# Two transformer blocks on one core: the unit after next rounded between the token tiles, and up products with channels on partitions

## What is computed

```python
def rmsnorm(x, w):
    xf = x.astype(jnp.float32)
    y = xf * lax.rsqrt(jnp.mean(xf * xf, axis=-1, keepdims=True) + EPS)
    return (y * w.astype(jnp.float32)).astype(x.dtype)

def conv_ffn(h, w_up, conv_w, conv_b, w_down):
    u = causal_depthwise_conv(h @ w_up, conv_w, conv_b)
    g, val = jnp.split(u, 2, axis=-1)
    return (jax.nn.silu(g) * val) @ w_down

def swiglu(h, w_gu, w_down):
    gate, up = jnp.split(h @ w_gu, 2, axis=-1)
    return (jax.nn.silu(gate) * up) @ w_down
```

## Time and profile before

| | |
|---|---|
| median of 3 runs | 998.97 us (998.82 to 999.09) |
| the profiled execution | 998.76 us |
| its span, first to last instruction | 997.0 us |
| TensorE, weight loads, VectorE, ScalarE, GpSimd busy | 98%, 82%, 62%, 52%, 7% |
| mean granted clock of TensorE | 0.998 |

### The profile page before, as it was taken

How to read it: one execution, slowest core, us unless ns; L and a number is a source line. 1 busy time by engine, 2 the same in 40 slices (tenths; PEclk the granted TensorE clock), 3 DMA queues, 4 the chain that set the end, 5 groups by cost and what they waited for, 6 DMA issues and landing times.

```text
span 997.0 us, 13465 instructions
## 1 busy us (share of the span) xinstructions
PE 975.3 (98%) x5011; PEld 821.8 (82%) x5011; DVE 616.8 (62%) x770; ACT 518.3 (52%) x748; POOL 66.9 (7%) x98
## 2 busy tenths in 40 slices
PE   7999999999999999999999999999999999999996
PEld 6888888787878888888788789999899878888885
DVE  5645454765665454556678787675553766666766
ACT  6443444565563434455458286545442475555555
POOL 3300000000100000000001623000000000000000
PEclk9999999999999999999999999999999999999999
DMA  9855555532446555555444333234652526465541
GB/s 322 279 190 190 184 195 177 203 126 106 124 150 213 194 185 185 193 172 186 169 156 148 117 130 127 85 127 147 231 172 85 169 89 235 141 205 173 180 157 43
DMA packets 110113, 166.01 MB, mean 167 GB/s; under 512 B 5684, under 2 KB 83796, under 8 KB 109940
## 3 DMA queue, kind: packets, MB, share of 16 engines
q1 hardware_dynamic: 108040, 160.45, 48.1%
q0 software_dynamic: 1872, 4.93, 1.5%
q10 hardware_dynamic: 160, 0.07, 0.0%
HBM read 164.38 MB, written 1.05 MB: 166 GB/s over the span
## 4 chain that ended last, share of the span: by engine, by line
PE 88%; ACT 4%; DVE 4%; POOL 2%; issue 1%; DMA 0%; POOLq 0%; ACTq 0%; DVEq 0%
PE ps L1988 26%; PE ps L1990 25%; PE ps L1989 25%; ACT w_hi L610 1%; DVE w_lo L1291 1%; ACT xT_hi L668 1%; PE ps L2298 1%; PE ps L2197 1%; PE ps L2204 1%; DVE arena L1755 1%; PE ps L2272 1%; PE ps L2012 1%; PE ps L2536 1%; ACT xs L640 1%; PE ps L2694 1%
## 5 line engine op out<-in xcount | busy, mean ns | idle before, releaser
L1291 DVE TENSOR_TENSOR w_lo<-raw,w_hi 128x2048 fp32r<-128x2048 f32 (+1 forms) x141 | 322.4, 2296 | 151.7 <-ACT w_hi L610 151.6
L1988 PE MATMUL ps<-w_hi,xT_hi 128*128 128x512 f32 (+2 forms) x898 | 349.2, 389 | 6.4 <-DVE w_lo L1291 2.6
L1990 PE MATMUL ps<-w_hi,xT_lo 128*128 128x512 f32 (+2 forms) x898 | 339.9, 379 | 0.0
L1989 PE MATMUL ps<-w_lo,xT_hi 128*128 128x512 f32 (+2 forms) x898 | 339.5, 378 | 0.0
L610 ACT ACTIVATE w_hi<-raw 128x2048 fp32r<-128x2048 f32 (+1 forms) x141 | 265.7, 1897 | 66.1 <-PE ps L1990 56.8
L1988 PEld LDWEIGHTS ps<-w_hi,xT_hi 128*128 128x128 f32 x898 | 169.2, 188 | 39.9 <-issue 4.5
L1990 PEld LDWEIGHTS ps<-w_hi,xT_lo 128*128 128x128 f32 x898 | 168.9, 188 | 32.2
L1989 PEld LDWEIGHTS ps<-w_lo,xT_hi 128*128 128x128 f32 x898 | 169.3, 189 | 30.6 <-issue 1.4
L1988 PE MATMUL ps<-w_hi,hT_hi 128*128 128x512 f32 x224 | 87.8, 392 | 0.0
L1989 PE MATMUL ps<-w_lo,hT_hi 128*128 128x512 f32 x224 | 87.4, 390 | 0.0
L1990 PE MATMUL ps<-w_hi,hT_lo 128*128 128x512 f32 x224 | 87.4, 390 | 0.0
(11 more groups left out here) (303 smaller groups left out, 1051.2 us busy)
## 6 DMA issues: line engine op xcount, KB each, us to landing
raw<-in_ffn_w_gu SPq DMA_DIRECT2D x86, 512.0 KB, 4.7
raw<-in_ffn_w_down SPq DMA_DIRECT2D x44, 512.0 KB, 3.9
raw<-in_w_ffn_up SPq DMA_DIRECT2D x44, 512.0 KB, 5.2
raw<-in_w_in SPq DMA_DIRECT2D x38, 512.0 KB, 4.7
raw<-in_w_out SPq DMA_DIRECT2D x24, 512.0 KB, 3.9
raw<-in_w_ffn_down SPq DMA_DIRECT2D x22, 512.0 KB, 4.4
raw<-in_w_mem_k SPq DMA_DIRECT2D x8, 512.0 KB, 4.0
raw<-in_w_mem_v SPq DMA_DIRECT2D x8, 512.0 KB, 4.7
```

The source lines that it names most:

```text
L1291: TTn(w_lo[HOME[k]][:, 0:n], raw[k % RING][:, 0:n], w_hi[HOME[k]][:, 0:n].bitcast(F32), ALU.subtract).then_inc(resid, 1)
L1988: pe.matmul(out_, lh, rh, start=first, stop=False, **kw)
L1989: pe.matmul(out_, lh, rl, start=False, stop=False, **kw)
L1990: return pe.matmul(out_, ll, rh, start=False, stop=last, **kw)
```

## The change

**Seams.** At the four seams the split of unit k+2 is taken from behind the wait for `rstd`. ScalarE does it between the squares of tile 0 and the eviction of tile 1, VectorE behind its part of tile 1. f0, the very first layer, stays. A one-column Silu is put on ScalarE ahead of wout's end.

**Convolution layer.** Chunk 0 stays. From chunk 1 on `conv_up` computes the up products with a 128x128 block of weights stationary and the 256 tokens moving, so the result has channels on partitions (channel blocks 0 and 2 in bank 0, 1 and 3 in bank 1) and no transposes follow. The factor now varies along the free dimension, so it is needed as a row on every partition: VectorE writes the two diagonals of `rstd` and a matrix of ones, TensorE multiplies them behind chunk 0's transposes (`factor_row`), ScalarE copies the row (`r_row`). VectorE multiplies banks 0 and 1 by the row into `u_s` (two instructions of 128x512 each chunk), and the taps read `u_s`. `gu_ps` is raised when bank 0 is complete, in the middle of the second unit. ScalarE's write of `hT_hi` now waits for the down products of the chunk before.

```diff
+                    if t == 0:
+                        split(U0[name] + 2)
...
                 squares(after, (0,))
+                split(U0[after] + 2)
                 turned_tile(after, 1)
...
-                if f or peeled != 0:
+                if peeled != 0:
                     split(k + 2, j)
...
-                for t in range(TT):
+                for t in range(TT if not conv or peeled == 0 else 0):
...
+                if conv and peeled == 0:
+                    act.wait_ge(r_ps, 1)
+                    act.activation(r_row, ps[:, 6, 0:S], ACT.Copy).then_inc(r_ready, 1)
...
+                    if n:
+                        act.wait_ge(unit_used, 3 * j + (k + 3))
                     act.activation(hT_hi[:, :, :], act_s[:, :, :], ACT.Copy).then_inc(hT_hi_done, 1)
...
+            act.activation(rec1[:, 0:1], neg_half[:, 0:1], ACT.Silu)
             post_and_norm("wout", "f1")
...
+                if conv and peeled == 0:
+                    nc.vector.tensor_scalar(ones, ident, 0.0, 1.0, ALU.mult, ALU.add).then_inc(diag_ready, 1)
+                    for t in range(TT):
+                        scale_rows(diag[:, t, :], ident, rstd[:, t, 0:1]).then_inc(diag_ready, 1)
...
+                    for p in range(2 if peeled != 0 else 0):
+                        if p == 0:
+                            dve.wait_ge(gu_ps, j + (fc + 1))
+                        else:
+                            dve.wait_ge(unit_used, 3 * j + (k + 2))
+                        TTn(u_s[:, p::2, :], ps[:, p, :].rearrange("p (a b) -> p a b", a=2), bh(r_row, 2),
+                            ALU.mult).then_inc(u_ready, 1)
...
+            def factor_row():
+
+                pe.wait_ge(diag_ready, 3)
+                pe.matmul(ps[:, 6, 0:S], ones, diag[:, :, :].rearrange("p a b -> p (a b)"), start=True,
+                          stop=True).then_inc(r_ps, 1)
+
+            def conv_up(k, j, c):
+
+                for half in range(2):
+                    pe.wait_ge(resid, 3 * j + (k + half + 1))
+                    for n in range(16):
+                        r, q = (n // 4, n % 4) if half == 0 else (n % 4, (0, 2, 1, 3)[n // 4])
+                        if half == 0 and n < 2 and c > 1:
+                            pe.wait_ge(u_ready, 2 * j + (2 * c - 3 + n))
+                        last = product(ps[:, q % 2, q // 2 * S:q // 2 * S + S], wt(k + half, 512 * r + P * q, P),
+                                       (xT_hi[:, 4 * half + r, :], xT_lo[:, 4 * half + r, :]),
+                                       half == 0 and r == 0 and q < 2, half == 1 and r == 3, skip_group_check=True)
+                        if half == 1 and n == 7:
+                            last.then_inc(gu_ps, 1)
+                    last.then_inc(unit_used, 1)
...
                 if conv:
                     turn(f, conv, 0, 0)
-                    gate_up(u + 2, 0)
+                    factor_row()
+                    conv_up(u + 2, 0, 1)
+                    pe.wait_ge(r_ready, 1)
...
                 down(u + 4, 0, n_hT + 1, True)
-                turn(f, conv, 0, 1)
+                if not conv:
+                    turn(f, conv, 0, 1)
...
                 if conv:
-                    pe.wait_ge(hT_lo_done, n_hT + NCH - 1)
-                    last_turn()
                     down(k9, 0, n_hT + NCH - 1, False)
                     pe.wait_ge(last_lo, 2)
```

More of the change, by code:

```diff
@@ L99 @@
 GROUPS = [("mla", g, (1, 2), 4, MV) for g in range(4)]
+MG = len(GROUPS)
 MEM_Q_BANK = (0, 1, 4, 5)
@@ L249, in two_blocks @@
         act_in = view(0, TT, 512)
+        u_s = view(0, 4, S)
+        r_row = view(3072, S)
+        diag = view(3328, TT, P)
+        ones = view(3584, P)
         conv_y = view(1024, 4, S)
@@ L752, in chunk @@
                     for p in range(2):
-                        act.wait_ge(uT_ps, NCH + p)
+                        act.wait_ge(u_ready, 2 * (NCH - 2) + p + 1)
                         for q in (p, p + 2):
-                            act.activation(conv_y[:, q, :], ps[:, LAST_BANK[q], 0:S], ACT.Identity,
+                            act.activation(conv_y[:, q, :], u_s[:, q, :], ACT.Identity,
                                            bias=conv_now[:, 6 + q // 2, q % 2:q % 2 + 1],
@@ L764, in chunk @@
                     n = fc - 2 * NCH
-                    act.wait_ge(uT_ps, j + (n + 1))
+                    if n == 0:
+                        act.wait_ge(uT_ps, 1)
+                    else:
+                        act.wait_ge(u_ready, 2 * j + 2 * n)
                     act.wait_ge(taps_ready, j + (n + 1))
                     for q in range(4):
-                        act.activation(conv_y[:, q, :], ps[:, 2 + q // 2, q % 2 * S:q % 2 * S + S], ACT.Identity,
+                        src = ps[:, 2 + q // 2, q % 2 * S:q % 2 * S + S] if n == 0 else u_s[:, q, :]
+                        act.activation(conv_y[:, q, :], src, ACT.Identity,
                                        bias=conv_now[:, 6 + q // 2, q % 2:q % 2 + 1],
@@ L954, in _ @@
                 c, b = IN2_CHUNKS[n], IN2_BANKS[n]
-                for i in range(2):
+                for i in range(1 if n == 0 else 0, 2):
                     split(in2_unit0(n) + i + 2)
@@ L1090, in mem_exps @@
             def mem_exps(h):
-                act.wait_ge(neg3_ready, h + 1)
+                act.wait_ge(negm_ready, 2 * MG + h + 1)
                 if h >= 2:
-                    act.wait_ge(pT3_ps, h - 1)
+                    act.wait_ge(pT_ps, MG + h - 1)
                 for t in range(TT):
@@ L1098, in mem_exps @@
                                           bias=neg3[:, c:c + 1], scale=MEMD ** -0.5, accum_out=sum3[:, c:c + 1])
-                last.then_inc(p3_ready, 1)
+                last.then_inc(p_ready, 1)
             def mem_out_hi(h):
@@ L1426, in last_tap @@
                                 dve.wait_ge(tap1, 4 * (NCH - 1) + 2 * p + i + 1)
-                            src = ps[:, LAST_BANK[q], 0:S]
+                            src = u_s[:, q, :]
                             STT(out=conv_y[:, q, back:S], in0=src[:, 0:S - back],
@@ L1455, in chunk @@
                         for q in range(4):
-                            dve.wait_ge(first_done, 4 * j + (4 * n + (q // 2 * 2 + 1 if tap == 1 else q) + 1))
-                            src = ps[:, 2 + q // 2, q % 2 * S:q % 2 * S + S]
+                            dve.wait_ge(first_done, 4 * j + (4 * n + (q // 2 * 2 + 1 if tap == 1 and n == 0 else q) + 1))
+                            src = ps[:, 2 + q // 2, q % 2 * S:q % 2 * S + S] if n == 0 else u_s[:, q, :]
                             STT(out=conv_y[:, q, back:S], in0=src[:, 0:S - back],
@@ L1950, in _ @@
             turned_tile("f2", 1)
+            split(U0["f2"] + 2)
             feed_forward(2, True)
@@ L2179, in end_turn @@
                 last.then_inc(end_hT_ps, 1)
-            def last_turn():
-                pe.wait_ge(u_ready, 2 * NCH)
-                for p in range(2):
-                    for t in range(TT):
-                        for q in (p, p + 2):
-                            last = pe.transpose(ps[:, LAST_BANK[q], t * P:t * P + P],
-                                                act_in[:, t, q * P:q * P + P], ident)
-                    last.then_inc(uT_ps, 1)
+            def factor_row():
[15 more added lines that the diff above has]
+                    last.then_inc(unit_used, 1)
             def turn(f, conv, j, c):
@@ L2719, in mem_weighted @@
                                          v3[:, kt, h * MEMD:h * MEMD + MEMD], start=(kt == 0), stop=(kt == 1))
-                last.then_inc(o3_ps, 1)
+                last.then_inc(o_ps, 1)
             def mem_turn_out(h):
-                pe.wait_ge(o3_ready, h + 1)
+                pe.wait_ge(o_ready, MG + h + 1)
                 if h:
```

69 lines of the change are left out of this document (39 added, 30 removed).

## The result

The changed kernel takes 989.97 us in the median of four runs (989.76 to 990.56), the kernel before, run beside it, 998.93 us (998.82 to 999.09). The ratio is 0.9913, with a 95% interval from 0.9901 to 0.9925: 9.0 us faster. The forecast was 990.4 us with a range from 988.9 to 993.8. The profiled execution took 989.96 us, with a span of 988.1 us.

The account below looks back on a forecast made before the run. TensorE, busy 98% of the span, was taken as the bound. Loop 1.6, seams 5.5 and end 1.5 us sum to 8.6, taking the span from 997.0 to 988.4 and the median to 990.4 us, range 988.9 to 993.8.

Parts of the forecast that it names:

- the loop: Convolution layer: narrow products without transposes, chunk 17.32 to 17.08 us; nine periods save 2.2 us.
- the first three seams: f0 to win, wout to f1, f1 to in2: earlier rounding of unit k+2 removes TensorE's stalls, saving 4.8 us.
- the end: End of convolution layer: early bank 0 and no transposes start the last taps sooner, saving 1.5 us (1.0 to 1.8).
- the seam to f2: Entry to convolution layer: one rounding left after the factor, next up products 809.1 instead of 809.79, saving 0.7 us (0.4 to 1.1).
- The tenth up run's 0.6: Convolution layer's last up run: narrow products give back 0.6 us, its dropped transposes being counted with the end.
- The cover: First three seams: ScalarE idle at least 1.96 us before second tile's eviction, rounding 1.8 to 1.9; VectorE idle 3.58, subtraction 2.29.
- The reason given for the table load at f1: Seam wout to f1: one-column Silu starts the 1.28 us table load early, in ScalarE's 2.88 us of idle time.
- absorbed further on: Rival, chance 0.11: stretches behind win and in2 swallow both seam gains, 2.9 us, giving 993.3 us.
- The moved rounding: Rival at the seams, chance 0.05: ScalarE's moved rounding holds up the second tile; seams give nothing, 995.9 us.
- VectorE as the bound: Rival in the convolution loop, chance 0.03: VectorE's loop reaches 18.6 us, costing 1.5 us in nine periods, 1004.1 us.
- Weight loads of 0.192 us: Rival in the convolution up runs, chance 0.01: weight loads exposed, products every 0.192 us, 74 us lost, 1064 us.
- exactly half: Rival in the convolution up runs, chance 0.03: narrow product costs half a wide one, another 5.7 us saved, 984.7 us.

Follow-up runs that it names:

- the pair of dummy products: Kernel before plus unused VectorE products behind f2's second tile: one 128x2048, both operands in SBUF, 1001.8 us; two 128x1024, one operand in PSUM, 998.81 us.
- the run with the late bank: Changed kernel, VectorE's first eviction in the convolution layer waiting for the whole up run instead of bank 0 alone: 991.11 us.
- the run with 2.20 us more in each chunk: Changed kernel plus one unused VectorE product of 128x2048 ahead of the taps in each of the eight convolution loop chunks: 994.94 us.
- the run with the two-SBUF dummy: Kernel before plus one unused VectorE product of 128x2048, both operands in SBUF, behind the second tile at f2: 1001.8 us.

## Why the prediction was right, and where it was not

**Time and sign.** 990.4 us was forecast, 989.97 measured, inside the range. The sum of the terms was 8.6 us against 9.0. That it comes so near is in part luck: the loop, the first three seams and the end were forecast too small, by 0.7, 0.3 and 0.2 us, and the seam to f2 too large by 0.8.

**The loop: right in kind, too small by 0.7 us.** The prediction took 17.08 us for a chunk; it is 16.98, and over nine periods, with the kernel before at 17.33 in the mean, 2.93 us instead of 2.2. The tenth up run's 0.6 is 0.63. The mis-sized term is the chunk after the change. It holds 11.54 us for the up products, where 11.51 was measured, and the whole 5.54 us of the old down products; these take 5.47 us now, so the 0.07 us belonged to the hand-over to the transposes, which are gone. The 0.10 us too much stands in nine periods, and the first of them is 0.19 us longer than the rest, because behind the row product the second narrow product starts 0.31 us after the first instead of 0.12.

**The first three seams: right.** 4.8 us were forecast (1.47, 1.85, 1.46), 5.12 measured (1.56, 1.96, 1.60). The idle time and the 0.16 us of overlap make nearly all of it. The cover held: ScalarE's second-tile eviction still starts right behind TensorE's transposes, and in the version with VectorE's half left behind the factor the gain is the same. The reason given for the table load at f1 was wrong in part: it needs no help.

**The seam to f2: the step that failed.** The prediction gave 0.7 us between 0.4 and 1.1; the changed kernel gave -0.11, so even the sign of this term was wrong. Its working took GpSimd's factor at the same time as before ("the factor is there at 804.46"), and priced VectorE's moved subtraction at nothing because VectorE was idle. It asked what waits behind the moved instruction, not which other engine runs during it. So the rounding ahead of the first eviction, forecast to end 0.56 us before the start of the last product (806.6 against 807.16), ended 0.76 us behind it (803.04 against 802.28). With that one instruction put back behind the factor the seam gives 0.74 us, near the 0.7 forecast, and the pair of dummy products shows the mechanism. The row at 257.38 of the kernel before could have warned of it. The Trainium skill, SBUF — State Buffer, section "Who interferes with whom", says that a VectorE instruction with two SBUF inputs contends with a GpSimd instruction that reads SBUF; the same page's section "Summary: rules for kernel authors" adds that the second one to issue is blocked until the first has finished. By that rule the addition, which starts 0.56 us into a subtraction of 2.28 us, is held for 1.7 us; the trace agrees: it takes 1.80 us in place of 0.22 and ends 0.08 us behind the subtraction, and it takes 0.22 us where the second operand lay in PSUM.

**The end: right, too small by 0.2 us.** 1.5 us forecast, 1.70 measured, split by the run with the late bank into 0.9 for the early first bank and 0.8 for the rest. The taps start 0.93 us behind the last up product where 1.1 was forecast.

**The rivals.** Nothing was absorbed further on: win to f1 and in2 to f2 are shorter by 1.56 and 1.60 us. The moved rounding did not hold up the second tile. VectorE as the bound did not come: its own loop is 15.0 us against the 15.4 of the prediction, and the run with 2.20 us more in each chunk shows both that the bound exists and that it lies 2.0 us away. The price of that rival, nine times what the loop is too long, was too low, though: there the loop is 0.2 us too long, and 5.0 us were lost, because the end pays for VectorE's lateness (2.6 us) and for the lower clock behind that wait (1.6 us). Weight loads of 0.192 us stay hidden under products every 0.120 us. The 1064 us of that rival count the dearer narrow form twice: the 7.4 us are taken against the old up run of 10.99 us, but the 990.4 hold one of 11.54 already; from there it is 6.9 us a run, 1059 us. The narrow product is not exactly half: 0.120 against 0.229.

## What to carry to other kernels

When an instruction is moved into the idle time of its engine, look at what every other engine does in that time. A VectorE instruction of which both operands lie in SBUF is not free while GpSimd does a small step of a chain that someone waits for; behind that step it costs the same and hurts no one. When two engines' halves of a step are moved together, move them one at a time: here ScalarE's half gave the whole gain at the seams, and VectorE's half only the loss at f2. An engine whose busy time grows without a new instruction is the place to look first, and in the kernel before, an instruction that takes longer at one place than at its others.

## What the runs showed of the hardware

- GpSimd's addition on 128x2 numbers took 1.79 to 1.81 us instead of 0.22 at all four seams, and 1.80 us behind a dummy product with two SBUF operands; with one operand in PSUM it took 0.22 us. The profile counts the blocked time as busy time of GpSimd, so no idle time and no releaser points to VectorE.
- It goes the other way too, in the kernel before: VectorE's subtraction of 128x1536 takes 1.76 us at 578.03, with GpSimd idle, and 3.45 us at 563.00, where it starts 0.51 us into a GpSimd product of two SBUF operands (562.49, 2.35 us). GpSimd's addition of 128x4 numbers that follows at 564.92 takes 1.63 us and ends 0.10 us behind that subtraction.
- Matmuls of 256 columns, each with its own load of a 128x128 weight block, run every 0.120 us while each load lasts 0.192 us, in ten chunks of 96, without a gap.
- Behind the full-precision row product the first narrow product stands 0.31 us ahead of the next one (804.98 to 805.29); behind down products it stands 0.12 us ahead (839.13 to 839.25).
- In the run with a dummy in each loop chunk TensorE's granted clock was 0.50 (1.2 GHz) from about 979.3 to 982.7 us, behind 3.23 us without a matmul. Behind 2.82 us in the run with the two-SBUF dummy and behind 1.54 us in the run with the late bank it stayed at 1.00 in the profiled executions.
